# Expert weights of two token tiles scattered by index into DRAM, in place of one-hot matmuls

## The reference

```python
def block(hb):
    n = hb.shape[0]
    q = (hb @ w_q).reshape(n, PEER_HEADS, 2, PEER_HALF)
    s = jnp.einsum('nhid,hikd->nhik', q, sub_keys).astype(jnp.float32)
    s_top, i_top = lax.top_k(s, PEER_TOPK)
    cand = s_top[:, :, 0, :, None] + s_top[:, :, 1, None, :]
    cand_idx = i_top[:, :, 0, :, None] * PEER_N_KEYS + i_top[:, :, 1, None, :]
    best, pos = lax.top_k(cand.reshape(n, PEER_HEADS, PEER_TOPK * PEER_TOPK), PEER_TOPK)
    idx = jnp.take_along_axis(cand_idx.reshape(n, PEER_HEADS, -1), pos, axis=-1)
    w = jax.nn.softmax(best, axis=-1)
    u = jnp.take(u_tab, idx, axis=0)
    act = jax.nn.gelu(jnp.einsum('nhkd,nd->nhk', u, hb).astype(jnp.float32))
    out = jnp.einsum('nhk,nhkd->nd', w * act, jnp.take(v_tab, idx, axis=0))
    return out.astype(hb.dtype)
```

## Time and profile before

| | |
|---|---|
| runs | 3327.04, 3332.48, 3336.77 us; median 3332.48 |
| profiled execution | 3330.09 us, span 3328.2 us, mean granted clock 0.977 |
| busy | PE 3233.2 us, DVE 2111.0, ACT 1189.1, POOL 177.3 |
| stage U, first to last GELU | 1960.7 to 2690.7 us |
| DMA | 520.83 MB, mean 156 GB/s |

### The profile page before, as it was taken

How to read it: one execution, slowest core, us unless ns; L and a number is a source line. 1 busy time by engine, 2 the same in 40 slices (tenths; PEclk the granted TensorE clock), 3 DMA queues, 4 the chain that set the end, 5 groups by cost and what they waited for, 6 DMA issues and landing times.

```text
span 3328.2 us, 43237 instructions
## 1 busy us (share of the span) xinstructions
PE 3233.2 (97%) x17902; PEld 2891.7 (87%) x17902; DVE 2111.0 (63%) x3762; ACT 1189.1 (36%) x1601; POOL 177.3 (5%) x137
## 2 busy tenths in 40 slices
PE   7998999999999999999999999999999999999998
PEld 7888887878788889988778788999999999999998
DVE  6446865747544434767634689796977356777775
ACT  2234233222223423555532233444445322222222
POOL 0000000000000000000000000000000012323230
PEclk9888999999999998999999999999999999999999
DMA  5232112232231242122233333555456678898884
GB/s 233 94 114 114 52 39 107 84 107 91 93 122 63 77 157 90 56 75 89 95 143 129 114 122 142 194 178 200 156 183 211 211 263 320 317 326 312 322 312 153
DMA packets 213764, 520.83 MB, mean 156 GB/s; under 512 B 12320, under 2 KB 143904, under 8 KB 178112
## 3 DMA queue, kind: packets, MB, share of 16 engines
q1 hardware_dynamic: 192944, 442.92, 36.9%
q0 software_dynamic: 18464, 67.15, 6.1%
q10 hardware_dynamic: 2160, 7.99, 0.6%
HBM read 437.23 MB, written 80.74 MB: 156 GB/s over the span
## 4 chain that ended last, share of the span: by engine, by line
PE 87%; DVE 7%; ACT 3%; issue 1%; DMA 1%; SPq 0%; DVEq 0%; ACTq 0%
PE bank L570 80%; PE bank L1233 2%; PE bank L634 1%; DVE wl L525 1%; ACT wh L518 1%; PE bank L2504 1%; PE bank L582 1%; PE bank L641 1%; PE bank L2513 1%; PE bank L1498 0%; DVE ub L3191 0%; DMA cst<-in_consts 0%; DVE acc L148 0%; SPq L3041 0%; DVE gv L3145 0%
## 5 line engine op out<-in xcount | busy, mean ns | idle before, releaser
L570 PE MATMUL bank<-hh,wh 128*128 128x512 f32 (+2 forms) x2512 | 946.5, 377 | 16.4 <-DVE wl L525 6.3
L570 PE MATMUL bank<-hl,wh 128*128 128x512 f32 (+2 forms) x2512 | 918.1, 365 | 0.0
L570 PE MATMUL bank<-hh,wl 128*128 128x512 f32 (+2 forms) x2512 | 917.0, 365 | 0.0
L525 DVE TENSOR_TENSOR wl<-ring,wh 128x2048 fp32r<-128x2048 f32 (+2 forms) x249 | 554.5, 2227 | 554.3 <-ACT wh L518 553.5
L518 ACT ACTIVATE wh<-ring 128x2048 fp32r<-128x2048 f32 (+2 forms) x249 | 463.4, 1861 | 876.0 <-PE bank L570 867.5
L570 PEld LDWEIGHTS bank<-hh,wh 128*128 128x128 f32 x2512 | 479.7, 191 | 84.4 <-issue 18.1
L570 PEld LDWEIGHTS bank<-hl,wh 128*128 128x128 f32 x2512 | 479.2, 191 | 63.3 <-issue 6.0
L570 PEld LDWEIGHTS bank<-hh,wl 128*128 128x128 f32 x2512 | 478.3, 190 | 61.3
L570 PE MATMUL bank<-ph,wh 128*128 128x448 f32 x1024 | 372.5, 364 | 5.3 <-DVE pl L3156 5.3
L570 PE MATMUL bank<-pl,wh 128*128 128x448 f32 x1024 | 371.0, 362 | 0.0
L570 PE MATMUL bank<-ph,wl 128*128 128x448 f32 x1024 | 369.5, 361 | 0.0
(11 more groups left out here) (516 smaller groups left out, 4346.4 us busy)
## 6 DMA issues: line engine op xcount, KB each, us to landing
ring<-in_v SPq DMA_DIRECT2D x68, 1024.0 KB, 9.3
ring<-in_u SPq DMA_DIRECT2D x64, 1024.0 KB, 5.1
gelu_spill<-gst SPq DMA_DIRECT2D x128, 224.0 KB, 2.1
weight_spill<-stage SPq DMA_DIRECT2D x28, 1024.0 KB, 8.4
gv<-gelu_spill SPq DMA_DIRECT2D x64, 448.0 KB, 4.6
wv<-weight_spill SPq DMA_DIRECT2D x64, 448.0 KB, 7.3
ring<-in_ada SPq DMA_DIRECT2D x24, 1024.0 KB, 4.9
ring<-in_wup SPq DMA_DIRECT2D x22, 1024.0 KB, 4.8
```

The costliest lines, as they stand in the source:

```text
L525: v.then_inc(v.e.tensor_tensor(wl[q % 2][:, 0:n], ring[k % 4][:, 0:n], wh[q % 2][:, 0:n].bitcast(F32), S_), s("parts"))
L570: ins = p.e.matmul(out, l, r, start=start and i == 0, stop=stop and i == len(pairs) - 1, skip_group_check=not check)
```

## The change

Tiles 1 and 2 (256 tokens) no longer go through one-hot matmuls. DVE makes for each of their choices a cell number in a DRAM table `weight_scatter` of expert by token (16.8 MB), and POOL adds the weights into the table by 256 indirect DMAs of 128 cells; the 16 of one head wait until those of the head before have landed, since two heads may choose the same expert. POOL clears the table in the FFN of the first block, with 16 DMAs of 1 MB from a tile of zeros. The early tiles are now 1 and 2, and their `top` come first; 64 of the 112 quads go; five groups of eight DVE operations in `top_ve` become one operation each; `Ah` and `Bh` have two buffers for three; 76 empty steps stand ahead of `start`, whose first step stays at half-step 221. `fetch` waits for the whole scatter and reads weights by four DMAs for one.

```diff
-    wd_ = nc.dram_tensor("weight_spill", (7, 64, 128, 2, 64), F32).ap()
+    wd_ = nc.dram_tensor("weight_spill", (3, 64, 128, 2, 64), F32).ap()
+    sw_ = nc.dram_tensor("weight_scatter", (64, 2, 128, 256), F32).ap()
...
-        Ah = [sb(f"Ah{j}", [128, 4, 128], F32, ar) for j in range(3)]
-        Bh = [sb(f"Bh{j}", [128, 4, 128], F32, ar) for j in range(3)]
+        Ah = [sb(f"Ah{j}", [128, 4, 128], F32, ar) for j in range(2)]
+        Bh = [sb(f"Bh{j}", [128, 4, 128], F32, ar) for j in range(2)]
...
         norm_ve(v, 2, x1, cc["lnmix"])
+        v.wait_ge(s("zw"), 256)
         end_ve(v)
...
-    EARLY = 2
+    EARLY, ORDER = (1, 2), (1, 2, 0, 3)
...
-        for h in range(8):
-            v.then_inc(tt(cand[:, h, :].rearrange("p (a b) -> p a b", a=16), bc(top[:, 2 * h, :], 16),
-                          rep(top[:, 2 * h + 1, :], 16), A_), s("ve"))
+        pairs = top[:, :, :].rearrange("p (h c) k -> p h c k", c=2)
+        v.then_inc(tt(cand[:, :, :].rearrange("p h (a b) -> p h a b", a=16),
+                      pairs[:, :, 0, :].unsqueeze(3).to_broadcast([128, 8, 16, 16]),
+                      pairs[:, :, 1, :].unsqueeze(2).to_broadcast([128, 8, 16, 16]), A_), s("ve"))
...
-            for h in range(8):
-                e3 = eq[:, h, :].rearrange("p (k a) -> p k a", k=16)
-                v.then_inc(tt(e3, bc(paf[:, c, 16 * h:16 * h + 16], 16), rep(C["iota"][:, 0:16], 16), ALU.is_equal),
-                           s("ve"))
+            places = eq[:, :, :].rearrange("p h (k a) -> p (h k) a", a=16)
+            v.then_inc(tt(places, bc(paf[:, c, :], 16), rep(C["iota"][:, 0:16], 128), ALU.is_equal), s("ve"))
...
+        if j in SCATTER:
+            x = SCATTER.index(j)
+            v.then_inc(tt(swt[x][:, :].rearrange("p (h k) -> p h k", h=8), w3, bc(red8[:, 1, :], 16), M), s("wsel"))
+            v.then_inc(stt(v.e, sel[:, 0, :], sel[:, 1, :], 128.0, sel[:, 0, :], M, A_), s("ve"))
+            v.settle()
+            v.then_inc(ts(v.e, sidx[x][:, :], sel[:, 0, :], 256.0, M, stok[:, x:x + 1], A_), s("scr"))
...
     def top_sy(y, j):
-        if j >= EARLY:
-            y.wait_ge(s("seld"), 2 * j)
+        if j not in EARLY:
+            y.wait_ge(s("seld"), 2 * ORDER.index(j))
...
+    def cleared_po(g):
+        arrive(g, 3)
+        g.then_inc(g.e.memset(zeros[:, :], 0.0), s("zr"))
+        g.wait_ge(s("zr"), 1)
+        flat_w = sw_.rearrange("i x b t -> (i x b t)").rearrange("(p n f) -> p n f", p=128, f=2048)
+        for n in range(16):
+            g.e.dma_start(flat_w[:, n, :], zeros[:, :]).then_inc(s("zw").sem, 16)
+
+    def scatter_po(g):
+        cells = sw_.rearrange("i x b t -> (i x b t)").unsqueeze(1)
+        g.wait_ge(s("zw"), 256)
+        for x, j in enumerate(SCATTER):
+            g.wait_ge(s("wsel"), x + 1)
+            g.wait_ge(s("scr"), x + 1)
+            for h in range(8):
+                if h:
+                    g.wait_ge(s("scat"), 16 * (128 * x + 16 * h))
+                for k in range(16 * h, 16 * h + 16):
+                    g.e.indirect_dma_start(cells, bass.IndirectOffsetOnAxis(sidx[x][:, k:k + 1], 0), swt[x][:, k:k + 1],
+                                           None, compute_op=ALU.add).then_inc(s("scat").sem, 16)
...
         for t, q in quads(j):
-            if t >= 3:
-                v.wait_ge(s("ab_mm"), t - 2)
+            if t >= 2:
+                v.wait_ge(s("ab_mm"), t - 1)
...
+        yield from top(1)
+        yield from top(2)
         yield from top(0)
-        for j in range(3):
-            yield from weave((hot(j), 1), (top(j + 1), 0.75))
+        yield from weave((hot(0), 1), (top(3), 0.75))
         yield from hot(3)
+        for _ in range(76):
+            yield
         yield from start
...
         if i < 3:
-            y.wait_ge(s("ab_mm"), 112)
+            y.wait_ge(s("ab_mm"), 48)
+            y.wait_ge(s("scat"), 4096)
...
-        y.e.dma_start(wv[i % 3][:, :, :, :].rearrange("p b x t -> p b (x t)"),
-                      wd_[:, i].rearrange("b i x t -> i b (x t)")).then_inc(s(f"gv{i % 3}").sem, 16)
+        w = wv[i % 3]
+        y.e.dma_start(w[:, :, 64:320], sw_[i].rearrange("x b t -> b x t")).then_inc(s(f"gv{i % 3}").sem, 16)
+        for b, c in enumerate((0, 320, 384)):
+            y.e.dma_start(w[:, :, c:c + 64], wd_[b, i]).then_inc(s(f"gv{i % 3}").sem, 16)
...
     def pool(e):
         g = Line(e)
+        cleared_po(g)
         gprep_po(g)
+        scatter_po(g)
         gather_po(g)
```

More of the change, by code:

```diff
@@ L461, in _build @@
         red8 = sb("red8", [128, 2, 8], F32, ar)
-        tops = [top, cols[:, 0:256].rearrange("p (n k) -> p n k", n=16), top, top]
-        tixs = [tix, cst[:, 256:512].bitcast(U32).rearrange("p (n k) -> p n k", n=16), tix, tix]
-        Ah = [sb(f"Ah{j}", [128, 4, 128], F32, ar) for j in range(3)]
-        Bh = [sb(f"Bh{j}", [128, 4, 128], F32, ar) for j in range(3)]
+        tops = [top, top, cols[:, 0:256].rearrange("p (n k) -> p n k", n=16), top]
+        tixs = [tix, tix, cst[:, 256:512].bitcast(U32).rearrange("p (n k) -> p n k", n=16), tix]
+        Ah = [sb(f"Ah{j}", [128, 4, 128], F32, ar) for j in range(2)]
+        Bh = [sb(f"Bh{j}", [128, 4, 128], F32, ar) for j in range(2)]
+        sidx = [sb(f"sidx{j}", [128, 128], U32, ar) for j in range(2)]
+        swt = [sb(f"swt{j}", [128, 128], F32, ar) for j in range(2)]
+        sdiag = sb("sdiag", [128, 128], F32, ar)
+        stok = sb("stok", [128, 16], F32, ar)
+        sb("past_scatter", [128, 368], F32, ar)
         stage = [sb(f"stage{j}", [128, 128, 64], F32, ar) for j in range(2)]
@@ L471, in _build @@
         gv = [sb(f"gv{j}", [128, 2, ND], F32, ar) for j in range(3)]
-        wv = [sb(f"wv{j}", [128, 7, 2, 64], F32, ar) for j in range(3)]
+        wv = [sb(f"wv{j}", [128, 2, ND], F32, ar) for j in range(3)]
         sb("past_choice", [128, 1936], F32, ar)
@@ L2863, in early_ve @@
         v.wait_ge(s("sco"), n + 1)
-        for j in range(2):
+        for j in EARLY:
             top16(v, tops[j][:, n, :], tixs[j][:, n, :], sall[:, IN_SALL[j], n, :], sr[:, 0:128])
@@ L2878, in score_ve @@
         end_ve(v)
-    EARLY = 2
+    EARLY, ORDER = (1, 2), (1, 2, 0, 3)
     def top_idle(j):
-        for _ in range((11 if j >= EARLY else 0) + 1 + 8 + 1 + 6 + 1):
+        for _ in range((0 if j in EARLY else 11) + 1 + 8 + 1 + 6 + 1):
             yield
@@ L2890, in top_sc @@
         w3 = sel[:, 2, :].rearrange("p (h k) -> p h k", h=8)
-        for _ in range((11 if j >= EARLY else 0) + 1 + 8 + 1 + 6):
+        for _ in range((0 if j in EARLY else 11) + 1 + 8 + 1 + 6):
             yield
-        a.wait_ge(s("wdf"), j + 1)
+        a.wait_ge(s("wdf"), ORDER.index(j) + 1)
         a.then_inc(a.e.activation(w3, w3, ACT.Exp), s("wex"))
@@ L2962, in top_sy, with scatter_ve @@
         yield from top_idle(j)
+    SCATTER, HOT = (1, 2), (0, 3)
     def quads(j):
-        return [(32 * j + q - 16, q) for q in range(16 if j == 0 else 0, 32)]
-    WST = 256, 192
+        return [(q - 16, q) for q in range(16, 32)] if j == 0 else [(16 + q, q) for q in range(32)]
+    WST = 128, 64
+    def scatter_ve(v):
+        v.then_inc(v.e.tensor_tensor(sdiag[:, :], ident, C["iota"], M), s("ve"))
+        v.settle()
+        v.then_inc(v.e.tensor_reduce(stok[:, 0:1], sdiag[:, :], AX.X, A_), s("ve"))
+        v.settle()
+        v.then_inc(ts(v.e, stok[:, 1:2], stok[:, 0:1], 128.0, A_), s("ve"))
+        v.settle()
+    def cleared_po(g):
[17 more added lines that the diff above has]
+                                           None, compute_op=ALU.add).then_inc(s("scat").sem, 16)
     def hot_pe(p, j):
@@ L2974, in hot_pe @@
         yield
-        p.wait_ge(s("wsel"), j + 1)
+        p.wait_ge(s("wsel"), ORDER.index(j) + 1)
         if j:
-            p.wait_ge(s("ijw"), j)
+            p.wait_ge(s("ijw"), 1)
         for c in range(3):
@@ L3119, in experts_ve @@
         next_low(v, "u", 0)
+        scatter_ve(v)
         together((u_ve(v), 1), (choose_ve(v), CHOOSE))
@@ L3457, in sync @@
         y.wait_ge(s("sco"), 16)
-        for j in (2, 3):
+        for j in (0, 3):
             y.e.dma_start(sd_[j], flat(sall[:, IN_SALL[j], :, :])).then_inc(s(f"ssp{j % 2}").sem, 16)
```

55 lines of the change are left out of this document (27 added, 28 removed).

## The result

| | median us | lowest to highest | runs | ratio to before, 95% |
|---|---|---|---|---|
| before | 3331.8 | 3327.0 to 3338.5 | 13 | |
| after | 3339.3 | 3332.7 to 3347.7 | 13 | 1.0025 (1.0017 to 1.0034) |

The change makes the kernel slower by a quarter of a per cent: inside the 0.3% that the prediction called the same, inside its range of 3276 to 3358, and 34 us above its 3305. The profiled execution of after took 3340.0 us, 3338.1 of them its span.

What follows compares the result with a forecast made beforehand. The prediction took the matrix engine PE to bound the kernel: 3330.1 us less 57.9 of removed matmuls plus 30.4 of added waits gave 3302.6, a median of 3305. Its own range was 3290 to 3322, its 8-in-10 range 3276 to 3358.

Steps and rivals of the forecast that it cites:

- the scatter's price: POOL, stage U: 256 adding DMAs at pitch 1.6 and 14 landings of 7.7, 518 us, end 2541, no cost.
- The place of SP: Stage U: SP reaches its wait for the scatter in fetch, at half-step 221, at 2569 us.
- row of tops: Stage U: top(1), top(2), top(0) without quads between; DVE 179.0 us, PE waits 31.5; total with hot(0) 35.0, loss 30.4.
- threshold of 2.2 us: Scatter: price per adding DMA, waits included, at which SP stands at fetch and PE behind it; from 2.3 no gain.
- Rival 1: Scatter late: SP stands at fetch, PE behind it; slower, 3358 us by the upper bound; chance 0.22.
- Removed from PE: Stage U: 64 quads of 0.895 us and two sets of three transposes go, saving 57.9 us.
- The reload gap: Row of tops: top(0)'s scores reload after top(2)'s lists, leaving DVE 3 to 6 us idle, taken as 4.
- the FFN's clearing: FFN: POOL writes 16.8 MB, 52 us at 320 GB/s; cost 0, bounds 0 and 5 us.
- stage V's 256-byte pieces: Stage V: smaller packets add at most 0.6 us of transfer a tile, 9.1 fits into 9.6; cost 0.
- Rival 2: Stage V becomes DMA-bound by dear 256-byte pieces: +42 us, 3347; chance 0.10.
- Rival 3: Stage U: DVE's row of tops costs nothing, 3275 us; chance 0.10.
- Rival 4: Stage U: the row of tops costs 50 to 60 us through reload, ACT's table changes and POOL's port, 3325 to 3335; chance 0.08.

Runs made afterwards that it cites:

- e3: Kernel after, with the scatter's DMAs writing their cells instead of adding: 3297.4 us, 0.9896 of before.
- e7: Kernel after with e4's spacing, e6's order and the fetch 20 steps (19 half-steps) later: 3272.4 us, 0.9825 of before.
- e5: Kernel after without the scatter's indirect DMAs and without the wait for them: 3295.4 us, 0.9898 of before.
- e4: Kernel after with 18 empty steps woven into top(2) and top(0), taken from the 76 ahead of start: 3339.4 us, 1.0028 of before.
- e6: Kernel after with the two tiles' sets of 16 scatter DMAs alternating, each tile with its own semaphore: 3298.6 us, 0.9908 of before.
- e1: Kernel after with 96 empty steps for 76 ahead of start, so the fetch stands 19 half-steps later: 3299.4 us, 0.9903 of before.

## Why the prediction was wrong, and where it was right

**The step that failed: the scatter's price.** "I take the middle, 1.6, and the full landing of 7.7, since adding reads as well: 518, end 2541. It is in time, at no cost, with some 45 us to spare." It took 595 us and ended at 2619. The place of SP came out right (2569 forecast, 2568.3 measured), in part by luck: the sum had 35 us of PE's waits, and some 28 were lost there (26.4 in the row of tops, 2.0 for `sel`). What made up for it no run shows; the transposes, for one, aren't in that sum. The threshold of 2.2 us for each DMA was right in kind, and 2.32 is over it. Rival 1, at a chance of 0.22, is what happened: SP at `fetch` and PE behind it. Its rule, 2619 - 2585 = 34 us on 3305, even gives 3339. That this is the measured median is in part luck: the late scatter cost 44 us, and the row of tops some 8 less than the sum had. The upper bound of 615 us held the truth, and the value was taken in the middle between bounds where the row nearest to the case (an indirect DMA beside DVE's work, 1.67 and pitch 1.98 in the earlier trace rows) lay above it.

Rows 10 were also misread. The prediction has two gathers of 0.93 and 0.94 us "beside DVE's `Ah` and `Bh` work", and sets them against the rule that DVE can hold POOL's issue. DVE's timeline in before, beside those two and beside the one of 1.67:

```profile
2564.52 0.69 DVE L3022 TENSOR_TENSOR Bh<-cst,ijw 128x512 f32<-128x512 f32 x1 [1.60 <-PE bank L570]
2565.13 1.11 DVE L3025 TENSOR_SCALAR Ah<-cst,ijw 128x128 f32<-128x128 f32 x4
2568.95 2.29 DVE L525 TENSOR_TENSOR wl<-ring,wh 128x2048 fp32r<-128x2048 f32 x1 [2.71 <-ACT wh L518]
...
2704.85 1.23 DVE L3191 SCALAR_TENSOR_TENSOR ub<-ub,hT 128x1024 f32<-128x1024 f32 x1
```

`Ah` ended at 2566.24. The gathers at 2566.32 and 2567.57 ran while DVE stood idle; the one at 2705.20 started inside a two-input operation and took 0.73 us more. Over the 128 gathers of before, 66 of the 67 that started inside a TENSOR_TENSOR or SCALAR_TENSOR_TENSOR took over 1.03 us (median 1.68, up to 1.94), and none of the 61 others did (0.93 to 1.01). The trace of before had the price.

The price, term by term:
- Issue: 1.55 us, the least of the 256, and 0.30 between two: pitch 1.85 for 1.6. Shown by e3 to be the adding: 0.97 without.
- Issues that take longer: mean 1.785, 0.235 above the least, 60 us over all. These are not spread evenly. POOL's and DVE's timelines in after, the same ten us (start, duration):

```profile
2060.30 3.04 POOL L3014 DMA_INDIRECT weight_scatter<-swt,sidx  x1 [0.30 <-issue]
2063.64 2.02 POOL L3014 DMA_INDIRECT weight_scatter<-swt,sidx  x1 [0.30 <-issue]
2065.97 2.02 POOL L3014 DMA_INDIRECT weight_scatter<-swt,sidx  x1 [0.30 <-issue]
2068.30 1.55 POOL L3014 DMA_INDIRECT weight_scatter<-swt,sidx  x1 [0.30 <-issue]
...
2059.63 2.28 DVE L532 TENSOR_TENSOR wl<-ring,wh 128x2048 fp32r<-128x2048 f32 x1
2061.95 2.29 DVE L2938 TENSOR_TENSOR s_<-paf,cst 128x2048 f32<-128x2048 f32 x1
2064.28 2.29 DVE L2942 TENSOR_TENSOR s_<-s_,cols 128x2048 f32<-128x2048 f32 x1
2066.60 2.29 DVE L2947 TENSOR_REDUCE sel<-s_ 128x128 f32<-128x2048 f32 x1
```

The first starts at 2060.30, inside an operation that ends at 2061.91, and takes 1.49 us more than 1.55 where 1.61 of that operation was left; the next two start 0.60 us before the ends of theirs and take 0.47 more; the fourth starts inside a reduce, which has one input, and takes 1.55. Over all 256: of 69 that started inside a TENSOR_TENSOR of DVE, 65 took over 0.1 us more than the least, together 56 of the 60 us; of the 187 others 4 did, 3 of them with such an operation starting within 0.17 us behind their start. In e3 it is 71 of 79, and 6 of 177 by 0.11 us at most. What is added is mostly the rest of DVE's operation less 0.12 us; the longest, 4.22 us, had a second two-input operation close behind the first. The Trainium skill ("SBUF — State Buffer", section "Who interferes with whom", and the section "SBUF: two separate sides" ahead of it) says that a DVE operation with two inputs in SBUF and a GpSimd operation that reads SBUF shut each other out, and whichever starts first keeps the port. The trace agrees for POOL, the one-input reduce too. It doesn't for DVE, which isn't held by the scatter: 40 of `wl` started inside an issue of the scatter and took 2.27 to 2.29 us, as the 10 others of that stretch did. The prediction had the port for two-port operations only, and left its size to the upper bound. No run took DVE's operations away with the scatter left, so this part rests on what falls together in the traces.
- Landing: 3.3 us for each of 14 waits, not 7.7. This term was too dear by 62 us, and hid that the issue was too cheap by 0.25 x 256 = 64; the long issues, 60, and some pauses of the sequencer (90.0 us for 256 x 0.30 = 77) had no term. 518 - 62 + 64 + 60 + 13 = 593, for the measured 595.

**Removed from PE: right.** 57.9 forecast; e7's stage U is 57.8 shorter than that of before, with 4.8 us of waits for 6.3. The 1.5 us less of waits are offset by some 1.5 us of lower clock in e7 (0.97 over 2100 to 2150 us; an estimate).

**The row of tops: right in kind, 8 us too dear.** DVE's row was to last 179.0 us from 1978.2; it lasted 174.4, to 2152.6. `top(1)` took 38.2 of its own as forecast (1978.2 to 2023.2, less three lows of 2.27). The reload gap was 0.7, not 4: the wait is in DVE's list as `top` for `s_`, 0.7 us, once. And 14 lows fell inside it, not 14.6. By the prediction's own formula, 174.4 - 142.0 - 5.5 = 26.9 us lost by PE; measured are 17.9 of waits and 8.5 by the lower clock, 26.4. The forecast had all of it as waits. "PE's waits near 35 us, nearly all between 1985 and 2125" is wrong by this, and PE lost time up to 2150 (busy 42.10 of the 50 us from 2100); and "stage U about 703" is 695.1 in e5, where the scatter is gone, 8 less. Of the 3.5 us for `hot(0)`, the waits for `sel` show 2.0.

**The row's loss was off the path.** In e4 some 20 of its 26 us were gone and the time was the same, so in after this loss cost nothing beyond the late scatter. It counts when the scatter is in time: e7 is 26 us under e6, of which e6's last 3.2 us of SP's wait are a small part.

**At no cost: right.** This holds for the FFN's clearing and for stage V's 256-byte pieces. Rival 2, of which the prediction said that it is right by the rule for pieces under 512 B, is out: the DMA share is 0.91, and the stretch after the last GELU took 638.3 for 637.5 us. Rival 3, the row of tops for nothing, is out for the order as it was changed; with e4's spacing it is nearly right. Rival 4's 50 to 60 is out: the reload costs 0.7, and POOL adds nothing (e5).

**Where the gain went.** 44 us went into PE's stop behind SP's wait at `fetch` and its restart, and 21.8 into the row of tops (26.4 for the 4.6 of before), together more than the 57.9: 730.0 - 57.9 + 44.1 + 21.8 = 738.0, 1 us short of the measured 739.2. These are shares of the longer stage U, not what each repair alone would give back: by e4, spacing the row alone gives nothing. The stop is 41.0 us: SP waited 50.2, the work in the buffers covered 28 of it (PE ran dry at 2596.2, not 2585), and from SP's release at 2619.0 to PE's next matmul another 18 passed with fifteen DMAs of three fetches ahead of the spill and the u load. With some 2.4 us of lower clock at the restart that is 43.4 of the 44.1.

## What to carry to other kernels

A wait that is put on a queue is priced by what stands behind it on that queue as much as by what it waits for: the same scatter cost 44 us with SP's wait at half-step 221 and 4 to 6 with it 19 half-steps later (medians of e1 and e5, and their stages U of 701.3 and 695.1 us). Where a new chain of hundreds of equal steps has a deadline, work out the price for each step at which it is missed; if that lies between the bounds (here 2.2, between 1.36 and 2.4 all in), the chain isn't "in time with 45 us to spare", it is open. Moving the deadline (e1) and shortening the chain (e6) gave back the same 40 us here, and the first is an edit of one number. And when a late chain sets the end, savings ahead of it measure as nothing (e4), though they are real once it is in time (e7).

## What the runs showed of the hardware

- An indirect DMA of 128 four-byte cells keeps POOL 1.55 us when it adds and 0.97 when it writes; with 0.30 between two, and 3.3 us at each wait for landing (2.32 all in, 2.13 with the waits for landing nearly gone).
- An issue on POOL that starts inside one of DVE's two-input operations ends later, mostly by what is left of that operation less 0.12 us, up to 4.2 us for 1.55 (65 of 69 in after, 4 of the 187 others; 56 us of the scatter's 595). Gathers do the same: 66 of 67 in before, none of the 61 others. DVE's `wl` took 2.27 to 2.29 us beside the scatter or not.
- PE's granted clock fell where it only had short waits: 0.93 of full over 2050 to 2150 us, with single waits of at most 5.9 us; with the waits spread and short (e7) it was 1.00, 1.00 and 0.97. After the long stop it was 0.50 (1.2 GHz for 2.4) when PE began again in 2630 to 2640, and 0.90 in the ten us after that: by these lines about 2.85 x 0.5 + 10 x 0.10 = 2.4 us lost (estimate).
- 16.8 MB of clearing raised the FFN's DMA share from 0.38 to 0.91 over 60 us and PE was busy 54.85 us for 54.49.
- 768 pieces of 256 B and 256 of 1 KB in a tile, for 896 of 512 B, raised the DMA share from 0.89 to 0.91.
